# Four dense products with one product of 512 columns for a weight tile's high part, and a PSUM bank for each output tile

## The chip, the cores and the metric

The kernel runs on one core of a Trainium2 chip. Its metric is the device time of one execution in microseconds (us). The core has TensorE (PE, the matmuls), VectorE (DVE), ScalarE (ACT), GpSimd (POOL) and SyncE (SP), which here starts the loads of the weights. PE accumulates into PSUM, which has eight banks of 512 f32 numbers a partition; only ACT and DVE read it here.

## The reference, cut to what matters

Two transformer blocks over 256 tokens of width 2048. The products of the change are the first block's output projection and first feed-forward product, and the second block's output projection and its gate and up products:

```python
# first block
y = jnp.concatenate([o_hg, o_gdn], axis=-1) @ w_out[l]              # out_1
x = x + gt_m * rmsnorm(y, post_mix_norm[l])
h = rmsnorm(x, pre_ffn_norm[l]) * (1.0 + sc_f) + sh_f
y = jnp.square(jax.nn.relu(h @ w_ff1[l])) @ w_ff2[l]                # ff_1, ff_2
...
# second block
h = h + g1 * (o @ w_out)                                           # out_2
u = rms_norm(h, norm_ffn_g) * (1.0 + sc2) + sh2
h = h + g2 * ((jax.nn.silu(u @ w_gate) * (u @ w_up)) @ w_down)      # gate_up, down
```

All of it is float32. The mixers of both blocks (linear attention, four kinds of attention) are left out here.

## The kernel before, in words

Everything is kept transposed: 128 features on the partitions, 256 tokens along the free dimension. A product in f32 precision is made of three fp32r products. Each weight w is split into a high part (ACT copies it to fp32r, L951) and a low part (DVE subtracts, L1030), the activations x likewise, and an output tile sums high x high, high x low and low x high.

`phase_split_product` does this for out_1, ff_1, ff_2, out_2, gate_up and down. A turn has two chunks of 512 output columns (CW), that is NT = 4 output tiles of 128; in the narrow phases (out_1, ff_1, out_2, gate_up: 2, 8, 2 and 11 turns) the chunks follow each other, each over KT = 16 k tiles in four groups of KG = 4. ff_2 and down are "wide": their groups alternate between the chunks. For each k tile (a row of products) PE does four products high x high (L1114), one for each output tile nt, and then for each nt one of high x low (L1118) and one of low x high (L1120), each of 256 columns. The stationary operand is the weight tile of 128 x 128, the moving one the 256 tokens.

An accumulator is half a bank: tile nt of chunk c lies in bank 2c + nt // 2. So chunk 0 has banks 0 and 1, chunk 1 banks 2 and 3, and PE works on one chunk while the other is emptied by `empty`: ACT squares and copies (out_1: L651, L3159) or does relu and square (ff_1: L3172, L3174), DVE adds to x (out_2: L3167), or ACT does silu for the gate chunk (L2162) and DVE multiplies for the up chunk (L2167). Banks 4 to 7 hold sums of squares, warm-up products and the modulation's sums. The semaphore `free[c]` counts emptied tiles, `tile_ready` and `parts_used` tell that tiles are done.

All queues are in order, and what stands where is written out by hand. ACT does the high part of group 4 (or of the next turn's group 0) ahead of emptying the chunk that ends before it, then goes on with group 5. DVE does the low parts, and between them steps of the modulation's vector-matrix product (`ada.step`, L273 and L277), whose weights POOL loads. The ring of raw weights holds two groups; SP loads a slot again when DVE has used it (`core.used`). The split parts of two groups are held (`depth` = 8 k tiles). Each phase is a block of its own, and the next one starts when all engines have left it. `entry` is the normalization ahead of ff_1 and gate_up, `leaving` the sums of squares at the end of out_1, ff_2, out_2 and down.

## Time and profile before

| | |
|---|---|
| three timed runs | 2907.84, 2915.93, 2917.32 us |
| median | 2915.93 us |
| span of the profiled execution | 2908.0 us; no other time of that execution is on record |
| mean granted PE clock | 0.971 of 2.4 GHz |
| PE, DVE, ACT, POOL busy | 2770.6, 1994.6, 1324.5, 457.9 us |
| the products of `phase_split_product` | 3 x 4672 matmuls |
| HBM | 217 GB/s over the span |

The profile is of one execution on the chip. A row of the timeline merges neighbouring instructions of a kind: its second number is the time from the first one's start to the last one's end, and x4 is their count. Matmuls overlap, so the time from start to start is the time that each costs, not its duration. Numbers in square brackets are the engine's idle time before the row and what ended it.

### The profile page before, as it was taken

How to read it: one execution, taken by the hardware profiler on the slowest of the kernel's cores; microseconds unless marked ns; L12 is line 12 of the kernel's file. 1: busy time of each engine (PE TensorE's matmuls, PEld its weight loads, DVE VectorE, ACT ScalarE, POOL GpSimd, SP SyncE). 2: the span in 40 equal slices, each digit the busy share in tenths (PEclk: the TensorE clock that was granted, in tenths of full speed). 3: DMA queues.
4: the chain of work that ended last, by engine and by line, in shares of the span. 5: the costliest groups of instructions: out<-in, count | busy, mean ns of one | idle time of the engine just before them, and what ended most of it. 6: DMA issues, size and time to landing. Idle time of an engine off the chain costs nothing. (4 is left out here: it accounts for less than half of the span.)

```text
span 2908.0 us, 54817 instructions
## 1 busy us (share of the span) xinstructions
PE 2770.6 (95%) x21925; PEld 2685.4 (92%) x21925; DVE 1994.6 (69%) x2748; ACT 1324.5 (46%) x2058; POOL 457.9 (16%) x580
## 2 busy tenths in 40 slices
PE   8799999987999999999999999998999999999998
PEld 8789999786989999999998988887989999999998
DVE  6768996886776666687887588786577644444554
ACT  1354446534454444444444455555343333434454
POOL 1002997110011111011111021220011000000000
PEclk7799999898999999999999999999999999999999
DMA  9767665543667787787883776674568765565553
GB/s 386 250 199 242 223 220 194 198 117 138 216 218 275 266 287 272 242 287 265 276 281 117 181 233 214 210 236 141 175 243 281 227 182 181 175 188 169 177 185 134
DMA packets 290944, 632.55 MB, mean 218 GB/s; under 512 B 31490, under 2 KB 52422, under 8 KB 290502
## 3 DMA queue, kind: packets, MB, share of 16 engines
q1 hardware_dynamic: 239120, 484.78, 50.5%
q0 software_dynamic: 40192, 142.63, 14.6%
q10 hardware_dynamic: 11446, 2.54, 0.6%
q8 instruction: 131, 2.15, 0.3%
q14 instruction: 55, 0.45, 0.0%
HBM read 627.77 MB, written 2.10 MB: 217 GB/s over the span
## 5 line engine op out<-in xcount | busy, mean ns | idle before, releaser
L1118 PE MATMUL accumulators<-h_parts,weight_parts 128*128 128x256 f32 x4672 | 1179.0, 284 | 8.0 <-DVE weight_parts L1030 8.0
L1120 PE MATMUL accumulators<-h_parts,weight_parts 128*128 128x256 f32 x4672 | 1177.1, 284 | 0.0
L1030 DVE TENSOR_TENSOR weight_parts<-weights,weight_parts 128x1024 fp32r<-128x1024 f32 x584 | 708.0, 1221 | 410.8 <-ACT weight_parts L951 410.3
L1118 PEld LDWEIGHTS accumulators<-h_parts,weight_parts 128*128 128x128 f32 x4672 | 902.0, 193 | 10.7 <-DVE weight_parts L1030 10.7
L1120 PEld LDWEIGHTS accumulators<-h_parts,weight_parts 128*128 128x128 f32 x4672 | 902.0, 193 | 0.0
L951 ACT ACTIVATE weight_parts<-weights 128x1024 fp32r<-128x1024 f32 x584 | 611.6, 1060 | 627.0 <-PE accumulators L1120 449.9
L1114 PE MATMUL accumulators<-h_parts,weight_parts 128*128 128x256 f32 x4672 | 757.4, 285 | 19.9 <-DVE h_parts L1017 9.5
L1114 PEld LDWEIGHTS accumulators<-h_parts,weight_parts 128*128 128x128 f32 x4672 | 648.8, 193 | 22.6 <-DVE h_parts L1017 9.8
L1438 PE MATMUL accumulators<-in_h_parts,in_weight_parts 128*128 128x256 f32 x1024 | 261.5, 287 | 15.8 <-DVE in_weight_parts L1759 15.6
L1440 PE MATMUL accumulators<-in_h_parts,in_weight_parts 128*128 128x256 f32 x1024 | 258.4, 284 | 0.0
L1598 ACT ACTIVATE in_weight_parts<-weights 128x512 fp32r<-128x512 f32 x256 | 157.2, 630 | 201.4 <-PE accumulators L1440 144.4
L1759 DVE TENSOR_TENSOR in_weight_parts<-weights,in_weight_parts 128x512 fp32r<-128x512 f32 x256 | 188.3, 748 | 75.2 <-ACT in_weight_parts L1598 74.5
L2628 PE MATMUL accumulators<-in_h_parts,in_weight_parts 128*128 128x256 f32 x1632 | 217.7, 288 | 12.2 <-DVE in_weight_parts L3013 6.5
L2628 PEld LDWEIGHTS accumulators<-in_h_parts,in_weight_parts 128*128 128x128 f32 x1632 | 203.6, 192 | 24.1 <-DVE in_weight_parts L3013 9.3
L1438 PEld LDWEIGHTS accumulators<-in_h_parts,in_weight_parts 128*128 128x128 f32 x1024 | 197.6, 193 | 21.1 <-DVE in_weight_parts L1759 20.9
L1440 PEld LDWEIGHTS accumulators<-in_h_parts,in_weight_parts 128*128 128x128 f32 x1024 | 197.8, 193 | 0.0
L2764 ACT ACTIVATE in_weight_parts<-weights 128x512 fp32r<-128x512 f32 (+6 forms) x224 | 120.5, 554 | 160.4 <-PE accumulators L2628 147.7
L1431 PE MATMUL accumulators<-in_h_parts,in_weight_parts 128*128 128x256 f32 x1024 | 176.0, 294 | 3.7 <-DVE in_h_parts L1629 3.7
L3013 DVE TENSOR_TENSOR in_weight_parts<-weights,in_weight_parts 128x512 fp32r<-128x512 f32 (+6 forms) x224 | 129.3, 594 | 71.9 <-ACT in_weight_parts L2764 71.0
L277 DVE SCALAR_TENSOR_TENSOR ada_sums<-ada_weights,c_act,ada_sums 128x512 f32<-128x512 f32 x224 | 160.2, 746 | 20.4 <-DMA ada_weights<-in_w_ada 16.1
L232 POOL DMA_DIRECT2D h_t<-in_ada_w x96 | 69.0, 719 | 639.6 <-DVE h_parts L847 243.9
L1431 PEld LDWEIGHTS accumulators<-in_h_parts,in_weight_parts 128*128 128x128 f32 x1024 | 142.4, 193 | 16.9 <-issue 12.6
(389 smaller groups left out, 2751.2 us busy)
## 6 DMA issues: line engine op xcount, KB each, us to landing
weights<-in_w_ff SPq DMA_DIRECT2D x256, 512.0 KB, 5.5
weights<-in_w_in SPq DMA_DIRECT2D x160, 512.0 KB, 5.0
h_t<-in_ada_w POOLq DMA_DIRECT2D x96, 512.0 KB, 6.5
weights<-in_ffn_w_gate SPq DMA_DIRECT2D x88, 512.0 KB, 4.5
weights<-in_ffn_w_up SPq DMA_DIRECT2D x88, 512.0 KB, 3.9
weights<-in_ffn_w_down SPq DMA_DIRECT2D x88, 512.0 KB, 4.0
weights<-in_w_out SPq DMA_DIRECT2D x64, 512.0 KB, 4.7
wide<-in_ada_w POOLq DMA_DIRECT2D x128, 256.0 KB, 4.1
```

The lines of the kernel that those rows point to most:

```text
L277: ins = nc.vector.scalar_tensor_tensor(out=acc, in0=w, scalar=number, in1=acc, op0=ALU.mult, op1=ALU.add)
L951: nc.scalar.activation(w[:, held:held + take, 0, :], core.ring[:, q % RING, k:k + take, :], ACT.Copy).then_inc(core.high_ready, take)
L1030: ins = nc.vector.tensor_tensor(w[:, held:held + take, 1, :], core.ring[:, q % RING, k:k + take, :], w[:, held:held + take, 0, :].bitcast( ...
L1114: nc.tensor.matmul(accs[nt], w[:, held, 0, cols[nt]], xk[:, 0, :], start=(first and nt % 2 == 0), stop=False, skip_group_check=True)
L1118: nc.tensor.matmul(accs[nt], w[:, held, 0, cols[nt]], xk[:, 1, :], start=False, stop=False, skip_group_check=True)
L1120: ins = nc.tensor.matmul(accs[nt], w[:, held, 1, cols[nt]], xk[:, 0, :], start=False, stop=(last and nt % 2 == 1), skip_group_check=True)
L1431: nc.tensor.matmul(acc(c, nt), w[:, k, 0, nt * P:(nt + 1) * P], x[:, kt, 0, :], start=(kt == 0 and nt % 2 == 0), stop=False, skip_group_ch ...
L1438: nc.tensor.matmul(acc(c, nt), w[:, k, 0, nt * P:(nt + 1) * P], x[:, kt, 1, :], start=False, stop=False, skip_group_check=True)
L1440: ins = nc.tensor.matmul(acc(c, nt), w[:, k, 1, nt * P:(nt + 1) * P], x[:, kt, 0, :], start=False, stop=(kt == KT - 1 and nt % 2 == 1), sk ...
L1598: nc.scalar.activation(w[:, k, 0, :], core.ring[:, g % RING, part, :], ACT.Copy).then_inc(core.high_ready, 1)
L1759: ins = nc.vector.tensor_tensor(w[:, k, 1, :], core.ring[:, g % RING, part, :], w[:, k, 0, :].bitcast(F32), ALU.subtract)
L2628: ins = nc.tensor.matmul(out, stationary[:, a], moving[:, b], start=(kt == 0 and i == 0 and j == 0), stop=(kt == KT - 1 and i == 2 and j = ...
```

## The change

In the narrow phases the high part of a weight tile meets both parts of x in one product of 512 columns, whose two results lie side by side in a bank: columns 0 to 255 (the main part, high x high) and 256 to 511 (the rest, high x low). The low part's product of 256 columns adds to the rest. Every output tile nt has bank nt, in both chunks. A chunk is emptied in two steps: one copies the rest to SBUF on ACT, the other adds the main part on DVE, and what was done out of PSUM before is then done on the sum in SBUF; in out_2 DVE adds both parts to x. PE waits at a chunk's first row, tile by tile, until the tile of the chunk before is emptied. The last chunk of out_1 and of out_2 keeps its three products of 256 columns (`with_rests`). `tile_ready` is signalled for three tiles a chunk, as each is done. The order of the rows is the old one to a chunk's end (`by_tiles = False`): four high products, four low ones. DVE's modulation steps of the group ahead of a chunk's emptying now follow the emptying. The wide phases wait at their start for all banks.

```diff
@@ -851,7 +851,144 @@
-def phase_split_product(nc, core, name, following, chunk_steps, ada=None, ada_turns=None, entry=None, leaving=None, late=None):
+class Eviction:
+    takes_rests = True
+    def __init__(self, nc, core, c):
+        self.nc, self.core, self.c = nc, core, c
+    def begin(self, tile_done, main, rest, rests0, chunks):
+        self.tile_done, self.main, self.rest = tile_done, main, rest
+        self.rests0, self.chunks, self.free0 = rests0, chunks, self.core.claimed[self.c]
+    def take_rest(self, act, i, nt, to):
+        self.tile_done(act, i, self.c, nt)
+        self.nc.scalar.activation(to, self.rest(nt), ACT.Copy).then_inc(self.core.rests_out, 1)
+    def add_main(self, dve, i, nt, to):
+        dve.wait_ge(self.core.rests_out, i * (self.chunks * NT) + (self.rests0 + NT * self.c + nt + 1))
+        self.nc.vector.tensor_tensor(to, self.main(self.c, nt), to, ALU.add).then_inc(self.core.free[self.c], 1)
+    def wait_added(self, eng, i, nt):
+        eng.wait_ge(self.core.free[self.c], i * NT + (self.free0 + NT + nt + 1))
...
+class ReluEviction(Eviction):
+    def on_act(self, act, i):
+        nc, core = self.nc, self.core
+        for nt in range(NT):
+            self.take_rest(act, i, nt, self.sums[:, nt, :])
+        for nt in range(NT):
+            self.wait_added(act, i, nt)
+            nc.scalar.activation(self.sums[:, nt, :], self.sums[:, nt, :], ACT.Relu).then_inc(core.relu_steps, 1)
+        for nt in range(NT):
+            tile = NT * self.c + nt
+            act.wait_ge(core.relu_steps, i * (2 * NT) + (tile + 1))
+            nc.scalar.activation(core.big[:, bass.ds(i * (2 * NT) + tile, 1), :], self.sums[:, nt, :].unsqueeze(1),
+                                 ACT.Square)
+    def on_dve(self, dve, i):
+        for nt in range(NT):
+            self.add_main(dve, i, nt, self.sums[:, nt, :])
...
+    def on_act(self, act, i):
+        pass
+    def on_dve(self, dve, i):
+        v = self.core.dve
+        for nt in range(NT):
+            self.tile_done(dve, i, self.c, nt)
+            v.mark(self.add_to_x(i, nt, self.main(self.c, nt)))
+        for nt in range(NT):
+            dve.wait_ge(v.sem, v.n - NT + nt + 1)
+            self.add_to_x(i, nt, self.rest(nt)).then_inc(self.core.free[self.c], 1)
...
+    def on_act(self, act, i):
+        for nt in range(NT):
+            act.wait_ge(self.gate_used, i * NT + (nt + 1))
+            self.take_rest(act, i, nt, self.gate[:, nt, :])
+        for nt in range(NT):
+            self.wait_added(act, i, nt)
+            self.nc.scalar.activation(self.gate[:, nt, :], self.gate[:, nt, :], ACT.Silu).then_inc(self.gate_ready, 1)
+    def on_dve(self, dve, i):
+        for nt in range(NT):
+            self.add_main(dve, i, nt, self.gate[:, nt, :])
...
+    def on_dve(self, dve, i):
+        for nt in range(NT):
+            self.add_main(dve, i, nt, self.sums[:, nt, :])
+        for nt in range(NT):
+            self.wait_added(dve, i, nt)
+            dve.wait_ge(self.gate_ready, i * NT + (nt + 1))
+            self.nc.vector.tensor_tensor(self.core.big[:, bass.ds(i * NT + nt, 1), :],
+                                         self.sums[:, nt, :].unsqueeze(1), self.gate[:, nt, :].unsqueeze(1), ALU.mult
+                                         ).then_inc(self.gate_used, 1)
+def phase_split_product(nc, core, name, following, last_step, evictions=None, ada=None, ada_turns=None, entry=None,
+                        leaving=None, late=None):
...
         def acc(c, nt):
+            if not wide:
+                return core.ps[:, nt, 0:SEQ]
             return core.ps[:, 2 * c + nt // 2, (nt % 2) * SEQ:(nt % 2 + 1) * SEQ]
+        def rest(nt):
+            return core.ps[:, nt, SEQ:2 * SEQ]
+        def with_rests(i, c):
+            return not wide and not (leaving and isinstance(i, int) and i == st.turns - 1 and c == chunks - 1)
         def tile_done(eng, i, c, nt):
-            if nt < 2:
-                eng.wait_ge(core.tile_ready, i * chunks + (tr0 + c + 1))
+            if nt < (2 if wide else NT - 1):
+                eng.wait_ge(core.tile_ready, i * (chunks * signals) + (tr0 + c * signals + (1 if wide else nt + 1)))
             else:
                 eng.wait_ge(core.parts_used, row_tile(i, last_group[c] + 1, 0))
+        for e in evictions or ():
+            e.begin(tile_done, acc, rest, core.rests_n, chunks)
         def empty(eng, which, i, c):
-            on, step = chunk_steps[c]
+            if with_rests(i, c):
+                if which == "act":
+                    evictions[c].on_act(eng, i)
+                else:
+                    evictions[c].on_dve(eng, i)
+                return
+            on, step = last_step
             if on == which:
                 for nt in range(NT):
                     tile_done(eng, i, c, nt)
...
-                        n, slots, at = (ada.per_turn * KT, KG * (st.unit - 1 - start) // take,
-                                        (KG * (q - start) + k) // take)
-                        for s in range(n * at // slots, n * (at + 1) // slots):
...
             done, last = 0, st.turns - 1
             if entry:
...
+            def group(i, q):
+                c = q // per_chunk
+                two = with_rests(i, c)
+                by_tiles = False
+                every_k, every_nt = list(range(KG)), list(range(NT))
+                batches = [(every_k, [nt]) for nt in every_nt] if by_tiles else [([k], every_nt) for k in every_k]
+                for n, (ks, nts) in enumerate(batches):
+                    for k in ks:
+                        kt, held = place(q, k)[1], (KG * q + k) % depth
+                        if n == 0 or not by_tiles:
+                            parts_ready(i, q, k)
+                        for nt in nts:
+                            if kt == 0:
+                                if isinstance(i, int) and i + c == 0:
+                                    pe.wait_ge(core.free[0], f0[0] + NT)
+                                pe.wait_ge(core.free[1 - c], i * NT + (f0[1 - c] + NT * c + nt + 1))
+                            high = w[:, held, 0, nt * P:(nt + 1) * P]
+                            if two:
+                                nc.tensor.matmul(core.ps[:, nt, :], high, x[:, kt].rearrange("p a t -> p (a t)"),
+                                                 start=(kt == 0), stop=False, skip_group_check=True)
+                            else:
+                                for part in range(2):
+                                    nc.tensor.matmul(acc(c, nt), high, x[:, kt, part, :], start=(kt == 0 and part == 0),
+                                                     stop=False, skip_group_check=True)
+                    for k in ks:
+                        kt, held = place(q, k)[1], (KG * q + k) % depth
+                        if n == 0 or not by_tiles:
+                            pe.wait_ge(core.used, i * (HALVES * st.unit) + (HALVES * (st.first + q) + k // take + 1))
+                        for nt in nts:
+                            ins = nc.tensor.matmul(rest(nt) if two else acc(c, nt), w[:, held, 1, nt * P:(nt + 1) * P],
+                                                   x[:, kt, 0, :], start=False, stop=(kt == KT - 1),
+                                                   skip_group_check=True)
+                            if nt == NT - 1:
+                                ins.then_inc(core.parts_used, 1)
+                            elif kt == KT - 1:
+                                ins.then_inc(core.tile_ready, 1)
             def turn(i):
+                    if not wide:
+                        group(i, q)
+                        if late and i == 0 and q == 0:
+                            late.sums(pe)
+                        continue
                     for k in range(KG):
...
                         pe.wait_ge(core.high_ready, row_tile(i, q, k) + 1)
                         for nt in range(NT):
                             if first and nt % 2 == 0:
+                                if i == 0:
+                                    pe.wait_ge(core.free[1 - c], f0[1 - c] + NT)
+                                    pe.wait_ge(core.free[c], f0[c] + NT)
...
                              {(1, 3): (8, [(0, 4, 4)]), (1, 6): (12, [(0, 8, 4), (0, 2, 2), (0, 1, 1)])}, (1, 7))
-        phase_split_product(nc, core, "out_1", "ff_1", on("act", into_squared(y, y_squares)),
-                            ada=[(w_ada, 0, 18, 1)], leaving=y_squares)
+        phase_split_product(nc, core, "out_1", "ff_1", ("act", into_squared(y, y_squares)),
         entry = Entry(nc, core, after_out_1, C_PREFFN, 0, 3 * KT, 4 * KT, XSquares(nc, core, after_out_1, 0, {}, {}),
-                      y_squares, y, C_POSTMIX, 2 * KT)
-        phase_split_product(nc, core, "ff_1", "ff_2", on("act", square_relu), ada=[(w_ada_2, 1, 0, 1)], entry=entry)
+                      y_squares, y, C_POSTMIX, 2 * KT, core.ps[:, 0:4, 0:SEQ])
+        with ExitStack() as ff_ctx:
+            sums = ff_ctx.enter_context(nc.sbuf_tensor("ff_sums", [P, NT, SEQ], F32))
...
```

## Rows read from the trace of the kernel before

**Rows 1.** The page: busy us of each engine, share of the span, instructions.

```profile
PE 2770.6 (95%) x21925; PEld 2685.4 (92%) x21925; DVE 1994.6 (69%) x2748; ACT 1324.5 (46%) x2058; POOL 457.9 (16%) x580
```

**Rows 2.** Groups by line, whole kernel: instructions, busy us, mean ns, idle before them.

```profile
L1118 PE MATMUL accumulators<-h_parts,weight_parts 128*128 128x256 f32 x4672 | 1179.0, 284 | 8.0 <-DVE weight_parts L1030 8.0
...
L1114 PE MATMUL accumulators<-h_parts,weight_parts 128*128 128x256 f32 x4672 | 757.4, 285 | 19.9 <-DVE h_parts L1017 9.5 <-ACT weight_parts L951 7.2 <-DVE h_parts L847 3.3
...
L951 ACT ACTIVATE weight_parts<-weights 128x1024 fp32r<-128x1024 f32 x584 | 611.6, 1060 | 627.0 <-PE accumulators L1120 449.9 <-DMA weights<-in_w_ff 110.1 <-DMA weights<-in_w_out 30.7
```

**Rows 3.** Timeline of PE inside ff_2: start us, duration us, engine, line.

```profile
1401.04 0.64 PE L1114 MATMUL accumulators<-h_parts,weight_parts 128*128 128x256 f32 x4
...
1402.48 0.64 PE L1114 MATMUL accumulators<-h_parts,weight_parts 128*128 128x256 f32 x4
```

**Rows 4.** Timeline of PE in the mixer: wider products; the last row is plain f32.

```profile
1599.98 1.28 PE L2628 MATMUL accumulators<-in_weight_parts,in_h_parts 128*128 128x408 f32 x6
...
1601.45 1.28 PE L2628 MATMUL accumulators<-in_weight_parts,in_h_parts 128*128 128x408 f32 x6
...
1868.90 2.88 PE L2628 MATMUL accumulators<-in_weight_parts,in_h_parts 128*128 128x320 f32 x18
...
1940.83 4.55 PE L2628 MATMUL accumulators<-in_h_parts,in_weight_parts 128*128 128x256 f32 x36
...
2017.62 1.88 PE L3057 MATMUL accumulators<-wide,ones 128*128 128x512 f32 x4
```

**Rows 5.** Timeline of PE and ACT at a chunk's end in ff_1.

```profile
1004.71 0.28 PE L1120 MATMUL accumulators<-h_parts,weight_parts 128*128 128x256 f32 x1
...
1005.03 0.37 ACT L3172 ACTIVATE accumulators<-accumulators 128x256 f32<-128x256 f32 x1 [1.73 <-PE accumulators L1120]
...
1005.31 0.64 PE L1114 MATMUL accumulators<-h_parts,weight_parts 128*128 128x256 f32 x4
1005.52 0.39 ACT L3174 ACTIVATE wide<-accumulators 128x256 f32 x1
```

**Rows 6.** Timeline of ACT and DVE emptying banks, in out_1, gate_up and out_2.

```profile
767.38 0.38 ACT L3159 ACTIVATE wide<-accumulators 128x256 f32<-128x256 f32 x1
...
768.96 0.46 ACT L3159 ACTIVATE wide<-accumulators 128x256 f32<-128x256 f32 x1
...
2401.82 1.07 DVE L2167 TENSOR_TENSOR wide<-accumulators,gate 128x256 f32 x3
...
2059.36 1.66 DVE L3167 SCALAR_TENSOR_TENSOR x_t<-accumulators,modulation,x_t 128x256 f32<-128x256 f32 x4 [2.88 <-PE accumulators L1120]
```

**Rows 7.** Timeline of DVE and PE where PE waited for DVE.

```profile
2148.58 1.22 DVE L1030 TENSOR_TENSOR weight_parts<-weights,weight_parts 128x1024 fp32r<-128x1024 f32 x1
...
2149.85 0.39 PE L1118 MATMUL accumulators<-h_parts,weight_parts 128*128 128x256 f32 x1 [0.35 <-DVE weight_parts L1030]
```

**Rows 8.** Longer idles of PE and their clock; windows end PEclk, DMA share, GB/s.

```profile
860.33 0.58 PE L1118 MATMUL accumulators<-h_parts,weight_parts 128*128 128x256 f32 x1 [2.18 <-DVE weight_parts L1030]
2163.87 0.54 PE L1118 MATMUL accumulators<-h_parts,weight_parts 128*128 128x256 f32 x1 [2.01 <-DVE weight_parts L1030]
1891.76 0.98 PE L2628 MATMUL accumulators<-in_h_parts,in_weight_parts 128*128 128x256 f32 x6 [1.37 <-ACT wide L2667]
2163.80:2167.00 3.20, 3.13 (x15) 3.13 (x16) 2.33 (x3) 1.06 (x1) 0.00 (x0) 0.52 1.02 381
1860.00:1920.00 60.00, 56.10 (x411) 50.54 (x410) 48.78 (x90) 34.42 (x95) 12.89 (x24) 1.00 0.72 230
```

**Rows 9.** Timeline of PE at the starts of ff_2 and of down.

```profile
1194.18 0.93 PE L1114 MATMUL accumulators<-h_parts,weight_parts 128*128 128x256 f32 x4 [4.15 <-ACT weight_parts L951]
...
2635.12 1.23 PE L1114 MATMUL accumulators<-h_parts,weight_parts 128*128 128x256 f32 x4 [3.03 <-ACT weight_parts L951]
```

**Rows 10.** Timeline behind the eviction of rows 5: DVE, then PE.

```profile
1009.44 1.22 DVE L1030 TENSOR_TENSOR weight_parts<-weights,weight_parts 128x1024 fp32r<-128x1024 f32 x1 [4.88 <-ACT weight_parts L951]
...
1011.55 0.28 PE L1118 MATMUL accumulators<-h_parts,weight_parts 128*128 128x256 f32 x1
```

119 lines of the change are left out of this document (82 added, 37 removed).

## Prediction

> **What bounds the kernel now.** I read the engines' line of the page first [rows 1]: TensorE (PE) is busy 95% of a span of 2908.0 us, at a mean clock of 0.971, VectorE (DVE) 69%, ScalarE (ACT) 46%. "Busy" of a pipelined matmul can hide gaps, so next came the groups by line and the waits of PE [rows 2]: the three dense lines L1114, L1118 and L1120 hold 4672 products each, and in all of them together PE sat idle some 28 us. Where the change acts, nothing but PE's own pace sets the end; ACT and DVE wait for PE far longer (L951 449.9 us) than PE for them. The timeline then gives the pace [rows 3]: a row of twelve products of 256 columns (one k tile, four output tiles) starts every 1.44 us, 120 ns a product, row after row. So each nanosecond that a product costs or saves there, and each stall at the end of a chunk, goes straight into the span. DMA is busy too, but no PE wait in these rows names it.
>
> **The amounts.** Four products are rebuilt: out_1 (2 turns), ff_1 (8), out_2 (2), gate_up (11), with two chunks a turn: 46 chunks of 16 rows. The last chunk of out_1 and of out_2 keeps its three products of 256 columns, so 44 chunks are new: 704 rows, 2816 pairs of a wide and a narrow product. ff_2 and down only get waits.
>
> **Gain: two products where there were three.** Columns stay 768 an output tile and k tile; what goes is one product's fixed part. At 2.4 GHz, 256 columns take 106.7 ns and the row shows 120, so 13.3 ns are fixed. No product of this type with 512 columns is in the trace. The nearest is the mixer's of 408 [rows 4]: six of 408 and three of 256 repeat every 1.47 us, so one of 408 takes (1.473 - 0.360)/6 = 185.5 ns: 170 by its columns and 15.5 fixed. In the same stage 36 products of 256 take 4.55 us, (4.55 - 0.28)/35 = 122 ns, 15.3 fixed. The fixed part does not shrink with width. I take 185.5 + 104/2.4 = 228.8 ns. A pair falls from 240 to 228.8, a row from 1.44 to 1.395 us, a chunk by 0.72 us; 2816 x 11.2 ns = **31.5 us gained**. Bounds: 320-column products run 18 in 2.88 us, the last 0.305 long, so 151.5 ns each and 18 ns fixed [rows 4]; 213.3 + 18.2 gives 231.5 and 24 us gained. From the other side: plain f32 products stream their columns twice, and four of 512 take 1.88 us, so with the last one's own 0.59 taken off (1.88 - 0.59)/3 = 0.430, or 215 ns for each 512 columns [rows 4]; that would be 25 x 2816 = 70 us. The 408 row is nearest in type and width, so it decides.
>
> The Trainium skill ("TensorE: Matmul & The Clock Gate", Back-to-back issue gap) gives N/2.4 + 2.5 ns for products back to back, 215.8 ns at 512 columns and 109.2 at 256. This trace does not agree at 256 (120) nor at 408 (185.5 against 172.5). By the rule at 512 alone the gain would be an estimated 68 us.
>
> **Cost: the banks are no longer doubled.** Before, chunk 0 used banks 0 and 1 and chunk 1 banks 2 and 3, so PE went on while the old chunk was emptied: in [rows 5] the next chunk starts 0.60 us after the last chunk's product for tile 1, without a gap. Now both chunks use banks 0 to 3, and the first product for tile nt waits until ACT has copied that tile's rest and DVE has added its main part. The row order is kept, so the four tiles finish only 120 ns apart, at the very end. Let S be the start of the last row's first low product; unstalled, the next chunk would start at S + 0.48 and its first four wide products end at S + 0.48 + 4 x 0.229 = S + 1.39.
> - ACT starts 0.04 us after the product ends [rows 5], at S + 0.28 + 0.04 = S + 0.32. A copy out of PSUM takes 0.38 and independent ones follow at 0.265 (six steps in 1.58) [rows 6]: the copies end at 0.70, 0.97, 1.23, 1.50.
> - DVE: an addition is priced as the multiplication of the same shape, out of PSUM: 0.416 us, three in 1.07, so one each 0.33 [rows 6]. After 0.04 us: starts 0.74, 1.07, 1.40, 1.72, ends 1.16 to 2.14.
> - PE restarts 0.05 us after DVE's end, and its first product is then 0.11 us longer (0.39 against 0.28) [rows 7], since its weights were not loaded ahead. Tile 0 goes at 1.21, the last at 2.14 + 0.05 + 0.11 = 2.30, and its 0.229 end at 2.53.
>
> So a boundary costs 2.53 - 1.39 = **1.14 us** against 0.72 gained in the chunk. Boundaries with this chain: 3 in out_1, 15 in ff_1, 21 in gate_up, 39 in all: **44.5 us**. Bounds: without the 0.11 it is 1.03 (40 us); with ACT's slowest copies of the rows (0.46) and a full weight load of 0.19 it is near 1.3 (51 us). In out_2 DVE does all eight steps: four main additions, then four rests, 0.395 apart (four in 1.66) and 0.476 long [rows 6]; only the rests free a tile: S + 0.32 + 7 x 0.395 + 0.476 + 0.05 + 0.11 + 0.229 = S + 3.95, a stall of 2.57, three times: **7.7 us**.
>
> **What the stall does to the clock.** An idle of 2.01 us at 2163.87 is followed by 3.2 us at 0.52 of the clock, so 3.2 x 0.48 = 1.5 us lost [rows 8]; an idle of 1.37 us leaves the stretch around it at 1.00 [rows 8]. The 39 boundaries hold PE idle for about 0.6 us and then in short pieces: no loss. Out_2's idle is about 1.8 us, between the two rows: half of 3 x 1.5, **2.3 us**; bounds 0 and 5.
>
> **The ends.** Leaving gate_up, DVE before did four multiplications after PE's end; now it finishes its additions at S + 2.14 and then multiplies, ending near S + 3.4, 1.9 us later; ACT starts the next phase's first part only when DVE too has left the block, and PE's 3.03 us idle waits for that part [rows 9]: **+1.9 us**. Leaving ff_1, the same 4.15 us idle hangs on ACT's last square [rows 9]: four copies, four relus, four squares twelve at 0.265 to 0.28 without the old gap of 0.12 between a relu and its square, take 3.3 us, as before; **+0.2**. The waits added in ff_2 and down are met by then.
>
> **Costed at nothing.** Behind ACT's eviction stands the next group's high part: DVE had made the low part from it at 1009.44 + 1.22 = 1010.66, 0.89 us before PE's first product with it at 1011.55 [rows 10]; ACT ends 0.2 later now, but PE comes 1.1 later, so the cover grows. DVE's sums moved behind its additions (2 or 3 of 0.67 us) end before that high part does. If this cover went, each late microsecond would count at all 39 boundaries. Turn 0 of ff_1 and of gate_up has idles of 2.18 and 2.01 us where DVE is late [rows 8]: DVE has 1.3 us more to do there, PE comes 1.1 us later to its wait by the stall and 1.4 us earlier by two chunks' gain: no change, bounds -4 (the idle and its slow clock vanish) and +3. Weight loads hang on DVE's low parts and have no new bound.
>
> **The sum:** -31.5 + 44.5 + 7.7 + 2.3 + 1.9 + 0.2 = **+25.1 us**, a span of 2933. The span is 7.9 us below the median of the three runs (its record has no other time around it), so the forecast is 2915.9 + 25.1 = **2941 us**, 0.9% slower.
>
> **Rivals.**
> 1. *The wide product hides its fixed part* (faster). If the 13 ns are the weight load showing behind 256 columns, it vanishes under 512: 215 ns, the plain f32 row. Gain 70, costs 57: -13.5, **2902**. For it: f32 rows; against: the 408 row, where it should have vanished already. It decides below 240 - 57/2.816 = 219.8 ns. 12%. The rule of the Trainium skill quoted above ("TensorE: Matmul & The Clock Gate") would bring this one.
> 2. *Both ends of the bounds favour it*: 222 ns (51 gained) and 1.0 us a boundary: about 0, **2916**. 17%.
> 3. *The stall is longer*: the evicting engines are held at the boundary (in [rows 5] ACT had been idle for only 1.73 us when it could begin), or group 5 comes late, 0.5 us more at 39 boundaries: +45, **2961**. 15%.
> 4. *The clock falls at the boundaries*: 1.5 us lost at the 39 as well: +59 over the forecast, **3000**. Against: the idle is far shorter than 1.37. 3%.
>
> The forecast's own case has 53%, from 2924 to 2956. Runs here tell from no change what is over 0.3% (8.7 us). Faster: rival 1 and little else, 0.11; within: rival 2 and an edge of the forecast, 0.18; slower 0.71. The range for 8 in 10 is 2908 to 2970: below lies most of rival 1, above the worst of 3 and 4.
>
> **What the profile after would show.** L1114's place taken by products of 512 columns, a row each 1.395 us; at each start of a chunk PE idle about 0.6 us, released by DVE's additions, and more before tiles 2 and 3; in out_2 about 1.8 us; PE idle in these lines of some 55 us (39 x 0.57 + 3 x 1.8 more) where there were 28; instructions on PE fewer by 2816. Wrong if a row takes under 1.36 us, or if the copy starts late after the last row because ACT or DVE is still at the previous group.

## The result

| | before | after |
|---|---|---|
| median of 4 runs | 2913.3 us (2907.84 to 2917.32) | 2952.74 us (2947.21 to 2955.24) |
| span of the profiled execution | 2908.0 us | 2945.4 us |
| mean granted PE clock | 0.971 | 0.972 |

The change makes the kernel slower by 1.3%: ratio 1.0134, 95% interval 1.0118 to 1.015. The forecast was 2941 us (2908 to 2970), +25.1; measured were +39.4 between the medians and +37.4 between the spans. Ratios here and below leave out slow runs; there was one, of the kernel with its last group by tiles (3921 us at a clock of 0.63).

The page of the kernel after, the engines' line and the two dense lines of the narrow phases (L1286 the product of 512 columns, L1297 that of the low part):

```profile
PE 2765.9 (94%) x19109; PEld 2537.1 (86%) x19109; DVE 2059.8 (70%) x2924; ACT 1364.6 (46%) x2210; POOL 455.6 (15%) x580
...
L1286 PE MATMUL accumulators<-h_parts,weight_parts 128*128 128x512 f32 x2816 | 788.9, 402 | 41.3 <-DVE h_parts L1174 9.5
...
L1297 PE MATMUL accumulators<-h_parts,weight_parts 128*128 128x256 f32 x2944 | 471.0, 282 | 5.5 <-DVE weight_parts L1187 5.3
```

PE has 2816 instructions fewer than in [rows 1], as counted, and about the same busy time. Its idle time ahead of the dense lines is 60.7 us (41.3 and 5.5 here, 13.9 on the others) where it was 27.9; the prediction had said some 55.

Two chunk ends in ff_1, the timeline of the kernel after, in the place of [rows 5]:

```profile
1019.96 0.64 PE L1297 MATMUL accumulators<-h_parts,weight_parts 128*128 128x256 f32 x4
1020.27 1.21 ACT L866 ACTIVATE ff_sums<-accumulators 128x256 f32<-128x256 f32 x4 [1.75 <-PE accumulators L1297]
1020.69 1.42 DVE L870 TENSOR_TENSOR ff_sums<-accumulators,ff_sums 128x256 f32<-128x256 f32 x4 [0.91 <-ACT ff_sums L866]
...
1021.17 1.50 PE L1286 MATMUL accumulators<-h_parts,weight_parts 128*128 128x512 f32 x4 [0.58 <-DVE ff_sums L870]
...
1022.50 0.64 PE L1297 MATMUL accumulators<-h_parts,weight_parts 128*128 128x256 f32 x4
...
1022.98 1.09 PE L1286 MATMUL accumulators<-h_parts,weight_parts 128*128 128x512 f32 x4
...
1042.63 1.09 PE L1286 MATMUL accumulators<-h_parts,weight_parts 128*128 128x512 f32 x4
...
1043.87 1.21 ACT L866 ACTIVATE ff_sums<-accumulators 128x256 f32<-128x256 f32 x4 [3.94 <-PE accumulators L1297]
```

Three things are to be read here. *The pace*: from the second row of a chunk (1022.98) to its sixteenth (1042.63) fourteen rows take 19.65 us, 1.4036 each, against 1.44 [rows 3] and 1.395 forecast. With 0.48 for the four narrow products, a wide one takes (1.4036 - 0.48)/4 = 230.9 ns, not 228.8. *The chain of a boundary*: with S = 1019.96, ACT copies from S + 0.31 (forecast 0.32), DVE adds from S + 0.73 (0.74), PE restarts at S + 1.21 (1.21), and the low products follow at S + 2.54 (2.53). *Its price*: ACT's copies of two chunks start 1043.87 - 1020.27 = 23.60 us apart; sixteen rows are 22.46; 1.14 us is the stall, as forecast. It holds for the others too: over all 36 boundaries of ff_1 and gate_up the last row of a chunk and the first of the next take together 1.15 us more than two rows inside a chunk (mean, starts of the first wide products in the trace).

The waits of PE after (waiting line, engine and line that ended the wait: us in total, times, longest):

```profile
PE accumulators L1652 <- DVE in_weight_parts L1973: 21.9, 17, 7.3
...
PE accumulators L1286 <- DVE ff_sums L870: 8.8, 15, 0.7
...
PE accumulators L1286 <- DVE gate L870: 6.6, 11, 0.7
PE accumulators L1286 <- DVE up_sums L870: 5.6, 10, 0.6
...
PE accumulators L1286 <- DVE x_t L930: 3.8, 2, 1.9
...
PE accumulators L1286 <- DVE wide L870: 3.0, 2, 2.3
```

15 chunks of ff_1, 11 and 10 of gate_up's: these are the boundaries, some 0.58 us idle each, and nothing in [rows 2] answers to them. The three waits of out_2 for x_t are 1.9 us each (the third stands on another line). The first line belongs to in_1, a phase that the change does not touch. Its longest wait is 7.3 us, and I come back to it.

Read from the timelines of both kernels, each of the four phases from its first product to PE's first one behind it (us):

| stretch | before | after | difference | forecast |
|---|---|---|---|---|
| start to out_1 | 695.2 | 704.6 | +9.4 | 0 |
| out_1 | 100.75 | 104.89 | +4.1 | +1.3 |
| ff_1 | 380.63 | 387.48 | +6.9 | +5.8 |
| out_2 | 97.49 | 104.72 | +7.2 | +7.9 |
| gate_up | 516.95 | 528.31 | +11.4 | +10.1 |
| norms, ff_2, in_2, down to the end | 1116.98 | 1115.4 | -1.6 | 0 |
| sum | 2908.0 | 2945.4 | +37.4 | +25.1 |

The four phases of the change cost 29.6 us where 25.1 were forecast. The other part of the gap, 9.4 us, lies ahead of every instruction that the change touches.

### The profile page after: what moved, and what is told of

Read it like the earlier page. It is cut to its first block and busy times, and to the rows that moved or that the text cites. A ratio compares the mean times of both kernels' runs of the same rounds, so it can differ in the third digit from the quotient of the medians.

```text
span 2945.4 us, 49916 instructions
## 1 busy us (share of the span) xinstructions
PE 2765.9 (94%) x19109; PEld 2537.1 (86%) x19109; DVE 2059.8 (70%) x2924; ACT 1364.6 (46%) x2210; POOL 455.6 (15%) x580
## 3 DMA queue, kind: packets, MB, share of 16 engines
q10 hardware_dynamic: 11446, 2.54, 0.5%
## 5 line engine op out<-in xcount | busy, mean ns | idle before, releaser
L1286 PE MATMUL accumulators<-h_parts,weight_parts 128*128 128x512 f32 x2816 | 788.9, 402 | 41.3 <-DVE h_parts L1174 9.5
L1286 PEld LDWEIGHTS accumulators<-h_parts,weight_parts 128*128 128x128 f32 x2816 | 486.1, 189 | 129.7 <-DVE ff_sums L870 10.9
L1297 PEld LDWEIGHTS accumulators<-h_parts,weight_parts 128*128 128x128 f32 x2944 | 451.2, 190 | 66.9 <-DVE weight_parts L1187 8.9
L1297 PE MATMUL accumulators<-h_parts,weight_parts 128*128 128x256 f32 x2944 | 471.0, 282 | 5.5 <-DVE weight_parts L1187 5.3
L1332 PE MATMUL accumulators<-h_parts,weight_parts 128*128 128x256 f32 x1728 | 435.8, 284 | 1.3 <-DVE weight_parts L1187 1.3
L1334 PE MATMUL accumulators<-h_parts,weight_parts 128*128 128x256 f32 x1728 | 435.3, 284 | 0.0
L1332 PEld LDWEIGHTS accumulators<-h_parts,weight_parts 128*128 128x128 f32 x1728 | 333.6, 193 | 1.9 <-DVE weight_parts L1187 1.9
L1334 PEld LDWEIGHTS accumulators<-h_parts,weight_parts 128*128 128x128 f32 x1728 | 333.6, 193 | 0.0
L1328 PE MATMUL accumulators<-h_parts,weight_parts 128*128 128x256 f32 x1728 | 280.0, 285 | 10.0 <-ACT weight_parts L1108 10.0
L1328 PEld LDWEIGHTS accumulators<-h_parts,weight_parts 128*128 128x128 f32 x1728 | 240.1, 193 | 10.4 <-ACT weight_parts L1108 10.4
L2833 PEld LDWEIGHTS accumulators<-in_h_parts,in_weight_parts 128*128 128x128 f32 x1632 | 203.3, 192 | 22.9 <-issue 8.7
L1652 PEld LDWEIGHTS accumulators<-in_h_parts,in_weight_parts 128*128 128x128 f32 x1024 | 199.8, 195 | 26.4 <-DVE in_weight_parts L1973 26.2
L1654 PEld LDWEIGHTS accumulators<-in_h_parts,in_weight_parts 128*128 128x128 f32 x1024 | 200.1, 195 | 0.0
```

Source lines behind the costliest of these rows:

```text
L1286: nc.tensor.matmul(core.ps[:, nt, :], high, x[:, kt].rearrange("p a t -> p (a t)"), start=(kt == 0), stop=False, skip_group_check=True)
L1297: ins = nc.tensor.matmul(rest(nt) if two else acc(c, nt), w[:, held, 1, nt * P:(nt + 1) * P], x[:, kt, 0, :], start=False, stop=(kt == KT ...
L1328: nc.tensor.matmul(accs[nt], w[:, held, 0, cols[nt]], xk[:, 0, :], start=(first and nt % 2 == 0), stop=False, skip_group_check=True)
L1332: nc.tensor.matmul(accs[nt], w[:, held, 0, cols[nt]], xk[:, 1, :], start=False, stop=False, skip_group_check=True)
L1334: ins = nc.tensor.matmul(accs[nt], w[:, held, 1, cols[nt]], xk[:, 0, :], start=False, stop=(last and nt % 2 == 1), skip_group_check=True)
L1652: nc.tensor.matmul(acc(c, nt), w[:, k, 0, nt * P:(nt + 1) * P], x[:, kt, 1, :], start=False, stop=False, skip_group_check=True)
```

## The experiments

All numbers of phases below are differences to the kernel before, read like the table above ("out_1 to ff_1" includes the norm between them). Times of the kernels with several rounds are medians beside the kernel before on the same chip.

**Undo the wide product alone.** Banks, waits and evictions stay as changed; the product of 512 columns becomes two of 256.

```diff
-  nc.tensor.matmul(core.ps[:, nt, :], high, x[:, kt].rearrange("p a t -> p (a t)"), ...)
+  nc.tensor.matmul(core.ps[:, nt, 0:SEQ], high, x[:, kt, 0, :], ...)
+  nc.tensor.matmul(rest(nt), high, x[:, kt, 1, :], ...)
```

> The kernel after, with each wide product undone: high x high into the main part and high x low into the rest as two products of 256 columns; banks, waits and evictions stay. In the profile after, a row takes 1.403 us, so a wide product costs 0.231 and the pair gains 9 ns against three products at 120. Theory (the wide product gains little, the boundary stall costs more): a row of 1.44 us, the boundary still 1.15 us over its rows, 2816 x 9 ns = +25 us against after, 2978 us, 2.2% over the kernel before. Rival 1 (the wide product brings most of its fixed part, the loss of the change is larger elsewhere): +70 us, 3022. Rival (the wide product brings nothing, the banks alone do it all): 2953.

Measured: 2967.54 us, ratio 1.0175 (1.0155 to 1.0195). The timeline of PE in ff_1, two rows of a chunk and the boundary:

```profile
1014.77 0.64 PE L1299 MATMUL accumulators<-h_parts,weight_parts 128*128 128x256 f32 x4
...
1016.21 0.64 PE L1299 MATMUL accumulators<-h_parts,weight_parts 128*128 128x256 f32 x4
1017.43 0.39 PE L1286 MATMUL accumulators<-h_parts,weight_parts 128*128 128x256 f32 x1 [0.58 <-DVE ff_sums L870]
...
1018.76 0.64 PE L1299 MATMUL accumulators<-h_parts,weight_parts 128*128 128x256 f32 x4
```

The row is back at 1.44 us, and the boundary is untouched: idle 0.58, low products 2.55 us after those of the last row. In the phases it is +22.0 (out_1 to ff_1), +11.6 (out_2), +22.1 (gate_up), together 55.7: 26.1 more than the changed kernel. The product of 512 columns is thus worth some 26 us (2816 x 9.1 ns = 25.6), and bank sharing costs 56. The row is the clean measure of it; that the sum of the phases agrees so well is in part luck. Ff_1 and gate_up give 18.1 us where their rows alone would give 22.1, and out_1 and out_2 give 8.0 where theirs would give 3.5, since the clock fell behind all three idles of out_2 here (one in the changed kernel) and out_1's first boundary had a longer idle (3.1 us for 2.3). The time rose by only 14.8 us between the medians, 10 less than expected, since out_1 begins at 694.28, 10.3 us earlier than in the changed kernel. So this run also shows that the lateness ahead of out_1 comes and goes with the later program.

**Let the tiles of the last row end apart.** Only the order of products within a chunk's last row changes: tile by tile, so that the first tile is ready 1 us ahead of the last.

```diff
+  if two and q % per_chunk == per_chunk - 1:
+      batches = batches[:-1] + [([KG - 1], [nt]) for nt in every_nt]
```

> The kernel after, with only the last of a chunk's 16 rows done tile by tile: wide, narrow, wide, narrow. The tiles then finish 0.351 us apart instead of 0.12. Theory (the stall is the chain product end, copy, addition, restart, of which only the last tile's is exposed): the last tile can start 1.21 + 0.11 us after its last narrow product starts, so 1.20 us after the chunk's end, where it is due at 0.69: a stall of 0.51 instead of 1.14, 39 x 0.63 = 25 us, out_2 about 2.5 less: 2926 us. Rival (the loss is the extra work on ACT and DVE, which holds up the next groups, not the wait for the banks): no change, 2953.

Measured: 2925.4 us, ratio 1.0032 (1.0020 to 1.0044). Timelines of two chunk ends in ff_1:

```profile
1013.05 0.40 PE L1288 MATMUL accumulators<-h_parts,weight_parts 128*128 128x512 f32 x1
...
1013.61 1.44 ACT L866 ACTIVATE ff_sums<-accumulators 128x256 f32<-128x256 f32 x4 [1.17 <-PE accumulators L1299]
...
1014.02 1.48 DVE L870 TENSOR_TENSOR ff_sums<-accumulators,ff_sums 128x256 f32<-128x256 f32 x4 [0.33 <-ACT ff_sums L866]
...
1014.50 0.19 PEld L1288 LDWEIGHTS accumulators<-h_parts,weight_parts 128*128 128x128 f32 x1 [0.19 <-DVE ff_sums L870]
...
1036.01 0.40 PE L1288 MATMUL accumulators<-h_parts,weight_parts 128*128 128x512 f32 x1
```

ACT and DVE now empty tile 0 while PE is in the same row, and the weight load for the next chunk's tile 0 waits only 0.19 us. A chunk takes 1036.01 - 1013.05 = 22.96 us against 22.46 for sixteen rows, so 0.50 of the stall is left. Phases: -0.1, +3.6, -0.1, together +3.4; 26.2 us are won without one instruction more or less. The end-of-chunk chain alone had given 0.51 for what is left, and work of ACT and DVE that holds them up would not have shrunk with the order: rival 3 was no part of the 1.14.

**The last group by tiles.** Four rows tile by tile, so that the tiles end 1.4 us apart.

```diff
-  by_tiles = False
+  by_tiles = two and q % per_chunk == per_chunk - 1
```

> The kernel after, with the last four rows of a chunk done tile by tile (sixteen products of one tile's bank, then the next). Tiles finish 1.4 us apart. Theory: the last tile's chain is the same as with the last row alone, so the same stall of 0.51: about 2923 to 2926 us. If it is the spacing of all tiles that matters (the chain is limited by ACT's and DVE's pace), it is clearly faster than the last row alone, below 2915. If the parts of four rows are not ready in time, it is slower, PE waiting for the high or low part at the start of a chunk's last group.

Measured: 2923.92 us, ratio 1.0032 (1.0019 to 1.0045). What is left of the waits for evictions of PE:

```profile
PE accumulators L1286 <- DVE gate L870: 2.7, 11, 0.3
...
PE accumulators L1286 <- DVE ff_sums L870: 2.5, 11, 0.2
PE accumulators L1286 <- DVE up_sums L870: 2.2, 9, 0.3
```

0.24 us at each of 31 boundaries. That is not the whole stall: a chunk takes 22.96 us (median of ff_1 and gate_up, from the starts in the trace), as with the last row alone, so 0.50 is left. The last tile ends as late as before, and the next chunk, still in rows, needs it within 0.7 us of its start. Phases: +2.5, +4.5, +1.7, together +8.7; no better than a single row by tiles.

**The first group by tiles too.** The next chunk then asks for tile 3 only after three tiles' work.

```diff
-  by_tiles = False
+  started = isinstance(i, int) and i + c == 0
+  by_tiles = (two and q % per_chunk == per_chunk - 1) or (q % per_chunk == 0 and not started)
```

> The kernel after, with the last four and the first four rows of a chunk done tile by tile, so that the next chunk needs the last tile's bank only 4.2 us after its start. Theory: no stall is left at the 39 boundaries and 1.2 us at out_2's three: 39 x 1.14 + 3 x 1.3 + 3 us of clock = -51 us, 2902 us, 0.4% under the kernel before, which is the wide product's gain of 25 us less the ends. Rival (the low parts of the first group are late: in the kernel before DVE had the second half of that group only 0.74 us ahead of the chunk): stalls of up to 1 us stay at each boundary where the loads are slow, 2915 to 2930 us.

Measured: 2908.54 us, ratio 0.9978 (0.9966 to 0.999). That is 6 us above the 2902 expected and under the rival's 2915. In ff_1 and gate_up the waits for evictions are gone but for one of 0.2 us. Phases: -5.5, +3.5, -10.2, together -12.3. In ff_1 and gate_up that is what the wide product gives when no boundary takes it back, less some loss at the changes of order. Out_1's first boundary still costs a wait of 2.07 us, and in out_2 this stands (timeline at the first boundary):

```profile
2040.53 2.01 ACT L1108 ACTIVATE weight_parts<-weights 128x1024 fp32r<-128x1024 f32 x2 [4.43 <-PE accumulators L1298]
2040.68 2.05 DVE L930 SCALAR_TENSOR_TENSOR x_t<-accumulators,modulation,x_t 128x256 f32<-128x256 f32 x5 [0.92 <-PE accumulators L1298]
2041.70 1.16 PE L1287 MATMUL accumulators<-h_parts,weight_parts 128*128 128x512 f32 x4 [1.06 <-ACT weight_parts L1108]
```

Three times PE waits 1.06 us at the phase's boundaries. The row names ACT's high part, because that one came last on the semaphore, but it is not the one that PE needs: it is the phase's eleventh, the next group's, and the ten that this group needs had ended at 2036.10. PE's product also waits for tile 0 to be free, and the addition of tile 0's rest, the second of the five at 2040.68, ended at 2041.56, 0.14 us before PE went on. So it is DVE, which adds all four main parts before the first rest, as expected. The next kernel tests this.

**DVE adds a tile's rest right behind its main part in out_2.** As tiles_both, but the second loop is gone: main and rest of tile 0, main and rest of tile 1, and so on.

```diff
         for nt in range(NT):
             self.tile_done(dve, i, self.c, nt)
             v.mark(self.add_to_x(i, nt, self.main(self.c, nt)))
-        for nt in range(NT):
-            dve.wait_ge(v.sem, v.n - NT + nt + 1)
+            dve.wait_ge(v.sem, v.n)
             self.add_to_x(i, nt, self.rest(nt)).then_inc(self.core.free[self.c], 1)
```

> The last and the first four rows of a chunk tile by tile, and in out_2 DVE adds a tile's rest right behind its main part instead of after all four. Theory: with both groups by tiles out_2's first product waits only for tile 0, but that came after all four main additions (S + 1.7); paired, tile 0 is free long before. out_2's three stalls of some 1.2 us go: 3 to 4 us less than both groups alone, 2905 us. If the clock had fallen in out_2 there, 1.5 us more for each time.

Measured: 2905.0 us, ratio 0.9955 (0.9941 to 0.9968): faster than both kernels. Its timeline at out_2's first boundary, without an idle of PE:

```profile
2044.45 3.73 DVE L930 SCALAR_TENSOR_TENSOR x_t<-accumulators,modulation,x_t 128x256 f32<-128x256 f32 x8
...
2046.85 1.09 PE L1286 MATMUL accumulators<-h_parts,weight_parts 128*128 128x512 f32 x4
2046.89 2.02 ACT L1107 ACTIVATE weight_parts<-weights 128x1024 fp32r<-128x1024 f32 x2 [4.42 <-PE accumulators L1297]
```

The next chunk begins at 2046.85, tile 0's rest having been added by 2045.45, and it begins before ACT starts on the piece that the row above had named.

Phases: -2.0, -0.3, -9.8, together -12.2. Out_2 is 3.8 us shorter than in tiles_both, but the first stretch is 3.5 longer, with three waits for ff_sums of 1.4 us in all; the two kernels' intervals overlap, so that only the end of the waits in out_2 is shown, not a gain of the whole.

**Both kernels once more**, for the lateness ahead of out_1.

> The kernel before, unchanged, for a second profile: out_1 started 9.4 us later in the profile after than in that of before, though nothing ahead of out_1 was changed (a load of the modulation's weights in the input product landed 4.5 us later, and PE stood 7.3 us there). If that is chance of the loads, the starts of out_1 scatter by several us in both kernels. If the change brings it, out_1 starts near 695 us again here.

> The kernel after, unchanged, for a second profile. If the late start of out_1 is chance, it is not tied to 704 us here; if the change brings it (the same code ahead of out_1 in another program), it is at 704 again. The boundary stalls and the row of 1.403 us are to be the same as in the first profile.

Measured: 2917.63 and 2949.28 us. Out_1 begins at 698.57 in the one and 703.62 in the other. In the phases both repeat within 1.5 us of the first profiles. Rows of the timeline at the place in in_1 where the two kernels part, first the kernel before, then the changed one (profiles of the first runs):

```profile
109.11 0.48 DVE L273 TENSOR_SCALAR attn_t<-scaled,c_act 128x512 f32<-128x512 f32 x1 [6.03 <-DMA scaled<-in_w_ada]
...
110.25 0.19 PEld L1438 LDWEIGHTS accumulators<-in_h_parts,in_weight_parts 128*128 128x128 f32 x1 [2.94 <-DVE in_weight_parts L1759]
```

```profile
112.65 0.49 DVE L273 TENSOR_SCALAR attn_t<-scaled,c_act 128x512 f32<-128x512 f32 x1 [10.54 <-DMA scaled<-in_w_ada]
...
113.79 0.29 PEld L1652 LDWEIGHTS accumulators<-in_h_parts,in_weight_parts 128*128 128x128 f32 x1 [7.50 <-DVE in_weight_parts L1973]
```

DVE waits for weights that POOL's queue loads (L273), 10.5 us instead of 6.0. DVE's low parts stand behind that wait, so PE idles 7.3 instead of 2.7 (its weight load, shown above, 7.50 and 2.94). The DMA views of 95 to 105 us in the same two profiles, queues with their packets, MB and share of the engines:

```profile
q0 software_dynamic: 265, 0.99, 26.9%
q10 hardware_dynamic: 1951, 0.12, 11.3%
q1 hardware_dynamic: 60, 0.23, 6.4%
```

```profile
GB/s 7 7 7 7 7 7 7 7 7 7 7 7 7 7 7 8 8 9 9 7 11 13 16 14 10 10 14 12 10 13 9 7 7 7 7 6 7 7 7 7
...
q10 hardware_dynamic: 1319, 0.08, 7.1%
```

In the kernel before, POOL's queue (q0) and SP's (q1) move 1.22 MB beside the small packets of q10 (64 bytes each, ACT's load of w_gates). In the changed kernel q10 alone moves anything, at some 8 GB/s. From some 107.5 us, when it is nearly through, the other loads run (up to 301 GB/s by 110 us), too late.

Up to this place the start is at 110.25 and 109.77 us in the two profiles of the kernel before, 113.79 and 116.25 in the two of the changed one. So the late loads are 3.5 us of the 9.4 between the first two profiles. From here to out_1 it is 585.0 and 588.8 against 590.8 and 587.4: that part differs by 3.4 to 3.8 between two runs of one kernel, more than the kernels' means (586.9 and 589.1) differ.

**Is it the length of the program?** 900 one-column products on PE (1800 instructions) in gate_up's entry, 2 ms after the place in question.

```diff
   keep_warm(self.nc, self.core, pe, 8 if self.y is None else 14)
+  if self.y is None:
+      for _ in range(900):
+          self.nc.tensor.matmul(self.core.ps[:, WARM_BANK, 0:1], self.core.ident[:], self.core.ones[:, 0:1], ...)
```

> The changed kernel with 900 one-column products added on TensorE at the entry of gate_up, long after out_1: nothing that runs before out_1 is altered, only the program that stands behind it is longer. Only the start of out_1 is read from it (the added products lengthen the whole kernel by some 40 to 90 us). If the later start of out_1 (703.6 to 705.2 in the kernels with wide products in tiles, 694.3 to 698.6 in the others) comes from how much TensorE program follows, out_1 should start here near 695 again, with attn_t's wait for the scaled weights back at about 6 us from 10.5. If it comes from something else in the changed kernel's program, out_1 starts near 704 as before and the wait stays 10.5.

```profile
108.95 0.48 DVE L273 TENSOR_SCALAR attn_t<-scaled,c_act 128x512 f32<-128x512 f32 x1 [6.22 <-DMA scaled<-in_w_ada]
```

The wait is back at 6.2 us, and PE restarts at 110.09. Out_1 begins at 699.61, 589.5 after that, so only the first part came back; 695 had been expected. The whole took 3326.85 us, since the added products cost 0.21 us an instruction at half the clock (0.50 from 2150 to 2500 us): some 380 us where I had expected 40 to 90.

**On another engine, or without products.** Both are tiles_both_paired with 900 waits on a semaphore that is long satisfied: on POOL, which has nothing left to do, and on PE behind down's last product.

```diff
+  if name == "down":
+      for _ in range(900):
+          pool.wait_ge(core.x_low, 1)      # pool_padded, in POOL's queue
+          pe.wait_ge(core.x_low, 1)        # pe_waits instead, at the end of PE's queue
```

> tiles_both_paired with 900 waits on a semaphore that is long satisfied, on POOL, behind its last load (POOL has nothing left to do from about 2310 us on), so that they cost nothing themselves. If the lateness upstream hangs on the length of the whole program, attn_t waits about 6 us for the scaled weights again instead of 10.5, TensorE's idle time there is 2.8 instead of 7.3, and the kernel takes some 4 us less than tiles_both_paired: ratio to before near 0.994. If it hangs on TensorE's program alone, the wait stays 10.5 and the ratio near 0.9955.

> tiles_both_paired with 900 waits on a semaphore that is long satisfied, on TensorE, behind the last product of down: the same count as the products that padded added, but without products, and at another place. Only the start of the kernel is read (the waits stand on the path near the end and lengthen it by an unknown amount). If it is the length of TensorE's program that counts, attn_t waits about 6 us for the scaled weights, as in padded (6.2). If it is its products, or the place, the wait stays 10.5.

POOL's program does nothing to it (10.54 in pool_padded; 2904.8 us, ratio to before 0.9967, 0.9953 to 0.9981); PE's does, halfway (8.27 in pe_waits; 2950.76 us as a whole, one run, with PE 47.5 us in the waits near its end). Set beside the packets by which the instruction queue q8 brings the program in: 123 packets go with 10.5 to 10.7 us (the changed kernel twice, the four kernels by tiles, pool_padded), 125 with 8.3 (pe_waits), 131 with 5.9 to 6.1 (before, narrow_again), 137 with 6.2 (padded). One kernel, pe_waits, stands between the two levels, so an order by length is only suggested. No packet of q8 runs between 95 and 105 us in either kernel, so a fetch in those 10 us is not what stands in the way.

## Why the prediction was right, point by point

- **Direction and mechanism** hold. PE's pace and the chunk ends decide; no other engine became the bound, and the low parts stayed ahead of the boundaries, as costed (PE waited for them four times on L1297, 5.3 us in all, never at a boundary). The direction does not hang on the lateness ahead of the change, since the four phases alone cost 29.6 us. But the size is part luck: 9.4 us of the 37.4 belong to no term of the sum, and the terms' own misses have both signs.
- **Gain, 31.5 us forecast: the term that was mis-sized.** The wide product takes 230.9 ns by the row, not 228.8: its fixed part is 17.6 ns, not the 15.5 of the product of 408 columns. The row is 36.4 ns shorter instead of 45, so 704 rows give 25.6 us, near the bound that I had from the products of 320 columns (24); undoing it cost 26.1. That this bound came near is luck, for its reading was wrong: the 18 products of 320 columns include a slow start (the second interval is 0.232 us). The nearest row was the right one to follow, but its period holds changes to and from 256 columns. Inside the groups, in the kernel before:

```profile
1601.64 1.09 PE L2628 MATMUL accumulators<-in_weight_parts,in_h_parts 128*128 128x408 f32 x5
...
1869.42 2.06 PE L2628 MATMUL accumulators<-in_weight_parts,in_h_parts 128*128 128x320 f32 x13
```

Thirteen products of 320, the last 0.305 long, start (2.06 - 0.305)/12 = 0.146 us apart, 13 ns beyond their columns and not 18. Those of 408 start 0.187 apart inside a group (five intervals from 1601.452 to 1602.388), 17 ns beyond; 0.187 + 104/2.4 would have given 230 ns for 512 columns. The far bound of 215 ns took each plain f32 instruction (0.430 us for 512 columns) for two passes over its columns, which no run here tests. The rule of the Trainium skill ("TensorE: Matmul & The Clock Gate", Back-to-back issue gap), 215.8 ns here, does not agree with the 230.9 measured; that section calls it the gap of an isolated product and gives about 131 ns at 512 columns for a stream of loads and products, which does not agree either. Rival 1, which stood on such a figure, is out, and so is rival 2, which needed 222.
- **Boundaries, 39 x 1.14:** exact where I measured it (1.14), step by step. With the gain set right, ff_1 should come to +8.0 and gate_up to +13.0; they came to 6.9 and 11.4. The boundaries are not cheaper for that (1.15 on the mean). The difference lies in turn 0 of both phases, which was costed at nothing (bounds -4 and +3): the idles of 2.2 us stayed, but the clock, which had fallen behind them before (0.52 at 2163.80 [rows 8], 0.57 from 860 to 864), did not fall this time. Windows of the kernel after (us from and to, length, busy of PE, PEld, DVE, ACT and POOL, PE clock, DMA share, GB/s):

```profile
874.00:878.00 4.00, 3.77 (x22) 3.38 (x23) 3.67 (x4) 1.06 (x1) 0.00 (x0) 1.00 1.01 378
2191.00:2195.00 4.00, 3.31 (x20) 2.97 (x21) 3.96 (x4) 1.07 (x1) 0.00 (x0) 1.00 1.03 386
```

That is the chance of an execution and not the change: in the second profiles it was the other way round in gate_up (1.00 behind the idle in the kernel before, 515.45 us; 0.52 in the changed one, 529.81 us). Alike in the clock, the two kernels differ by 12.9 us there (529.81 - 516.95, and 528.31 - 515.45), against the +13.0. In ff_1 the clock fell in both profiles of the kernel before and in neither of the changed one; padded, where it fell, has +7.7 there, against the +8.0.
- **Out_1, +1.3 forecast, +4.1 measured.** Here rival 3 happened, at one boundary. Timeline of the first one, and windows as above:

```profile
729.22 1.06 ACT L1108 ACTIVATE weight_parts<-weights 128x1024 fp32r<-128x1024 f32 x1 [2.42 <-DMA weights<-in_w_out]
...
730.31 1.23 DVE L1187 TENSOR_TENSOR weight_parts<-weights,weight_parts 128x1024 fp32r<-128x1024 f32 x1 [1.98 <-ACT weight_parts L1108]
731.45 1.41 DVE L870 TENSOR_TENSOR wide<-accumulators,wide 128x256 f32<-128x256 f32 x4
...
732.02 1.74 PE L1286 MATMUL accumulators<-h_parts,weight_parts 128*128 128x512 f32 x4 [2.31 <-DVE wide L870]
```

```profile
733.00:735.00 2.00, 2.00 (x8) 1.81 (x8) 1.89 (x3) 1.69 (x3) 0.51 (x1) 0.50 0.91 336
2056.00:2065.00 9.00, 7.97 (x42) 6.61 (x43) 6.04 (x10) 3.70 (x4) 0.00 (x0) 1.00 0.59 197
2108.00:2110.00 2.00, 2.00 (x11) 1.91 (x11) 2.00 (x3) 0.00 (x0) 0.00 (x0) 0.56 0.03 8
```

ACT's high part had waited 2.42 us for its load, so the low part of DVE stands at 730.31, ahead of the additions that free the banks. PE idles 2.31 us instead of 0.58, and the clock is at half (0.50) in the two microseconds behind. In last_row_by_tiles this wait is 1.9 and in tiles_at_end 1.5 us, but it is 1.8 in padded and 3.1 in narrow_again too, where the order is the one of the changed kernel: it goes with the loads of each execution, and no effect of the order can be read from it.
- **Out_2, +7.9 forecast, +7.2 measured.** The eight steps of DVE and PE's restart:

```profile
2054.83 3.23 DVE L930 SCALAR_TENSOR_TENSOR x_t<-accumulators,modulation,x_t 128x256 f32<-128x256 f32 x8 [1.85 <-PE accumulators L1297]
...
2057.03 1.58 PE L1286 MATMUL accumulators<-h_parts,weight_parts 128*128 128x512 f32 x4 [1.88 <-DVE x_t L930]
```

The steps take 3.23 us (forecast 7 x 0.395 + 0.476 = 3.24), and PE idles 1.88. The clock stayed at 1.00 behind this one; of the three, only the one of 1.95 us at 2107.07 was followed by a fall (0.56 in the window from 2108). In the second profile of the same kernel only the second fell, an idle of 1.88, and in narrow_again all three. I had charged half of 4.5 us.
- **The ends.** Ff_2 starts after this idle of PE:

```profile
1214.59 1.22 PE L1328 MATMUL accumulators<-h_parts,weight_parts 128*128 128x256 f32 x4 [5.04 <-ACT weight_parts L1108]
```

Down's is 4.97, as forecast (3.03 + 1.9) [rows 9]. Ff_2's is 5.04 against 4.15, 0.9 more where I had said 0.2: ACT's twelve steps take 3.63 us (1209.00 to 1212.63), and the eight before took 2.86 at this place (1189.35 to 1192.21), not the 3.3 that I had given both. The late low part in turn 0 of ff_1 and gate_up stayed (2.24 and 2.23 us) [rows 8].
- **Not forecast at all: +9.4 us ahead of out_1.** I took for granted that what stands before the change in time is not touched by it. Of it, 3.5 us are the late loads in in_1 (6.5 between the second profiles), which two profiles of each kernel repeat and which TensorE's later program switches: shown by padded, supported by narrow_again and pe_waits. The other 5.9 us lie in the stretch from there to out_1, which takes 584 to 591 us over all kernels and differs by up to 3.8 between two runs of one; what makes it up stays open. How the length or the place of TensorE's program acts on the order in which three DMA queues are served stays open; that it shifts where something lies in memory is a guess that no run here tested.

## What to carry to other kernels

Before two chunks share a bank, write out the chain from the last product to the next chunk's first (copy, addition, restart) and set it against how far apart the tiles end. Here 120 ns apart made 1.14 us of stall out of a 1.2 us chain, and one row in another order took half of that away for nothing. A saving in products needs such an order at both sides of the boundary before it shows. And compare the profiles at the first instruction that the change touches: a difference that is already there belongs to no step of the change's working, and it hid 10 us of what undoing the wide product costs. Where a phase comes out a microsecond or two off, look at the granted clock behind its idles in both profiles before the working is blamed.

## What was not expected of the hardware

- What an fp32r product costs beyond its columns grows here with width: 13 ns at 256 and 320 columns, 17 at 408 and 20 at 512 between starts inside a group (four of 512 take 1.09 us, the last 0.39 of it), 17.6 at 512 by the row.
- For ten microseconds a load of 64-byte packets on one queue ran while those of two others moved nothing (8 GB/s in all), and in padded, the same kernel with 900 products more on TensorE 2 ms later, it ran beside them (140 GB/s).
- Near 2 us the length of an idle of PE does not tell whether the clock falls. In the changed kernel's first profile idles of 1.88 (twice), 2.23 and 2.24 us left it at 1.00, and 1.95 and 2.31 us were followed by 0.56 and 0.50; in narrow_again idles of 1.88 (twice) and 1.95 us were all followed by 0.57 to 0.60.
